# Matmuls without a result in TensorE's waits between stages, and one PSUM bank kept out of the ring

## The reference

```python
def first_block(x, mem, ...):
    h = x
    for l in range(2):
        proj = rms_norm(h, norm_mix_pre[l]) @ w_in[l]
        ...  # dilated window attention, short convolution, gated delta rule
        mix = jnp.concatenate([y_attn, y_conv, y_gdn], axis=-1) @ w_out[l]
        h = h + rms_norm(mix, norm_mix_post[l])
        hn = rms_norm(h, norm_xattn_pre[l])
        xa = memory_cross_attention(hn, rms_norm(mem, norm_mem[l]), w_xq[l], w_xkv[l], w_xo[l])
        h = h + rms_norm(xa, norm_xattn_post[l])
        hn = rms_norm(h, norm_ffn_pre[l])
        h = h + rms_norm(swiglu_ffn(hn, w_gate_up[l], w_down[l]), norm_ffn_post[l])
    return h

def second_block(x, c, ctx, ...):
    for i in range(2):
        h_lat = rms_norm_2(x_lat, norm_g[i]) * (1.0 + sc_l) + sh_l   # the same for ctx
        ...  # i = 0: two grouped attentions; i = 1: conformer convolution and neighbourhood attention
        x_lat = x_lat + g_l * y_lat
    return rms_norm_2(x_lat, final_g)
```

## Time and profile before

| | us |
|---|---|
| median of three runs | 2859.71 (2857.09 to 2866.64) |
| profiled execution | 2864.18 |
| its span, first to last instruction | 2862.4 |
| PE busy | 2629.6 (92%) |
| DVE busy | 1673.3 (58%) |
| ACT busy | 1134.4 (40%) |
| mean clock granted to PE, of full speed | 0.941 |

### The profile page before, as it was taken

The page is one execution under the profiler, slowest core; times in us unless marked ns, Lnnn a source line. Parts: engine busy times, 40 slices in busy tenths (PEclk is TensorE's granted clock), DMA queues, the critical chain, the costliest instruction groups (busy, mean ns, idle before and its releaser), DMA issues.

```text
span 2862.4 us, 34696 instructions
## 1 busy us (share of the span) xinstructions
PE 2629.6 (92%) x13264; PEld 2107.0 (74%) x13264; DVE 1673.3 (58%) x3236; ACT 1134.4 (40%) x2071; POOL 0.2 (0%) x4
## 2 busy tenths in 40 slices
PE   7998899989999799898899899997989997899888
PEld 5876888668888578687876688886866666787556
DVE  6655565455446875565643644576376674398653
ACT  4235443433322332454444332323346673322562
POOL 0000000000000000000000000000000000000000
PEclk9989999989999899899999899996999998799898
DMA  4310033113226423101321232452110001122311
GB/s 146 99 52 16 2 118 111 43 65 98 96 98 220 139 81 99 38 1 45 120 87 57 69 96 96 161 192 92 52 37 16 23 16 33 34 81 67 69 43 45
DMA packets 73364, 218.33 MB, mean 76 GB/s; under 512 B 21232, under 2 KB 21488, under 8 KB 72560
## 3 DMA queue, kind: packets, MB, share of 16 engines
q1 hardware_dynamic: 48384, 176.29, 19.0%
q10 hardware_dynamic: 24816, 39.82, 4.4%
HBM read 213.98 MB, written 2.10 MB: 75 GB/s over the span
## 4 chain that ended last, share of the span: by engine, by line
PE 75%; DVE 13%; ACT 6%; issue 5%; DMA 1%; ACTq 1%; DVEq 0%; SPq 0%
PE bank L574 19%; PE bank L575 18%; PE bank L576 18%; PE bank L765 4%; PE bank L729 3%; DVE mod_part L2396 3%; PE bank L739 3%; ACT w_hi L533 2%; PE bank L1588 2%; PE bank L1183 1%; DVE w_lo L540 1%; PE bank L1191 1%; DVE hT L700 1%; PE bank L1129 1%; DVE y_x L693 1%
## 5 line engine op out<-in xcount | busy, mean ns | idle before, releaser
L574 PE MATMUL bank<-a_hi,w_hi 128*128 128x512 f32 (+1 forms) x1552 | 623.9, 402 | 43.5 <-ACT a_hi L603 21.7
L575 PE MATMUL bank<-a_lo,w_hi 128*128 128x512 f32 (+1 forms) x1552 | 613.1, 395 | 0.0
L576 PE MATMUL bank<-a_hi,w_lo 128*128 128x512 f32 (+1 forms) x1552 | 612.5, 395 | 0.0
L540 DVE TENSOR_TENSOR w_lo<-w_raw,w_hi 128x1024 fp32r<-128x1024 f32 x334 | 407.7, 1224 | 305.6 <-ACT w_hi L533 304.5
L533 ACT ACTIVATE w_hi<-w_raw 128x1024 fp32r<-128x1024 f32 x334 | 352.4, 1060 | 579.3 <-PE bank L576 486.5
L574 PEld LDWEIGHTS bank<-a_hi,w_hi 128*128 128x128 f32 (+1 forms) x1552 | 295.0, 190 | 132.6 <-issue 47.8
L576 PEld LDWEIGHTS bank<-a_hi,w_lo 128*128 128x128 f32 (+1 forms) x1552 | 295.1, 190 | 65.1
L575 PEld LDWEIGHTS bank<-a_lo,w_hi 128*128 128x128 f32 (+1 forms) x1552 | 295.2, 190 | 63.5 <-issue 3.0
L574 PE MATMUL bank<-b_hi,w_hi 128*128 128x512 f32 (+1 forms) x800 | 299.9, 375 | 36.0 <-DVE b_lo L713 23.5
L575 PE MATMUL bank<-b_lo,w_hi 128*128 128x512 f32 (+1 forms) x800 | 289.3, 362 | 0.0
L576 PE MATMUL bank<-b_hi,w_lo 128*128 128x512 f32 (+1 forms) x800 | 287.3, 359 | 0.0
(11 more groups left out here) (364 smaller groups left out, 3770.2 us busy)
## 6 DMA issues: line engine op xcount, KB each, us to landing
w_raw<-w_tiles SPq DMA_DIRECT2D x334, 512.0 KB, 3.4
mod_raw<-mod_tiles ACTq DMA_DIRECT2D x48, 512.0 KB, 3.5
d_bias<-rpb_rows ACTq DMA_DIRECT2D x16, 224.0 KB, 4.7
hT<-xT ACTq DMA_DIRECT2D x4, 512.0 KB, 11.2
m_in<-memT ACTq DMA_DIRECT2D x2, 1024.0 KB, 4.7
mod_cond<-cond_rows ACTq DMA_DIRECT2D x2, 1024.0 KB, 5.3
out<-hT ACTq DMA_DIRECT2D x8, 256.0 KB, 2.2
cT<-ctxT ACTq DMA_DIRECT2D x1, 1024.0 KB, 6.7
```

Of the source, the lines that this page charges most:

```text
L540: dve.tensor_tensor(w_lo[:, t % SPLIT, :], w_raw[:, t % RAW, :], w_hi[:, t % SPLIT, :].bitcast(f32), ALU.subtract).then_inc(sem("w_split"), 1)
L574: pe.matmul(o, wh, hi[:, k, :n], start=k == 0, stop=False)
L575: pe.matmul(o, wh, lo[:, k, :n], start=False, stop=False)
L576: mm = pe.matmul(o, wl, hi[:, k, :n], start=False, stop=k == kc - 1)
```

## The change

A helper `warm_pe(pe, n, key)` is added: it claims a bank, issues n plain f32 matmuls of 128 x 512 from two constant tables into it, and frees the bank itself with the last one; nobody reads the bank. It is called from twelve lines of PE's stream, 76 matmuls in all: in each of the two layers of the first block 1 ahead of the sums of `x_post`, 1 ahead of its broadcast, 5 behind it; 3 ahead of the sums of `f_post`, 1 ahead of its broadcast, and behind it 5 in layer 0 and 3 in layer 1; in the second block 3 ahead of the even input products, 9 ahead of the even attention, 13 ahead of the even output products, 3, 8 and 10 at the same places of the odd layer. Apart from this the bank of `rstd_pe` of `mix_post` is now held from its claim until product 11 of the memory has been issued.

```diff
+        def warm_pe(pe, n, *key):
+            b = claim(pe, "warm", *key)
+            for _ in range(n):
+                mm = pe.matmul(b[:, :], ident, con[:, 0:512], start=True, stop=True)
+            mm.then_inc(*freed("warm", *key))
...
-        def rstd_pe(pe, key, n):
+        def rstd_pe(pe, key, n, hold=False):
             pe.wait_ge(*when("spread", *key))
-            b = claim(pe, "rstd", *key)
+            b = claim(pe, "rstd", *key, hold=hold)
...
         def second_pe(pe):
             mod_norm_pe(pe, 0)
+            warm_pe(pe, 3, "even_in")
             even_in_pe(pe)
+            warm_pe(pe, 9, "even_att")
             attention_pe(pe, ("even",), even_units(), e_s, pair_tiles(e_pt), even_values,
...
+            warm_pe(pe, 13, "even_out")
             even_out_pe(pe)
             mod_norm_pe(pe, 1)
+            warm_pe(pe, 3, "odd_in")
             odd_in_pe(pe)
             conformer_pe(pe)
             odd_turn_pe(pe)
+            warm_pe(pe, 8, "odd_att")
...
+            warm_pe(pe, 10, "odd_out")
...
                 if c == 2:
-                    rstd_pe(pe, ("mix_post", l), S)
+                    rstd_pe(pe, ("mix_post", l), S, hold=True)
+                if c == KC + 3:
+                    book.release("rstd", "mix_post", l)
...
+                warm_pe(pe, 1, "x_post", l)
                 ssq_pe(pe, ("x_post", l), S)
+                warm_pe(pe, 1, "x_rstd", l)
                 rstd_pe(pe, ("x_post", l), S)
+                warm_pe(pe, 5, "f", l)
                 ffn_pe(pe, l)
+                warm_pe(pe, 3, "f_post", l)
                 ssq_pe(pe, ("f_post", l), S)
+                warm_pe(pe, 1, "f_rstd", l)
                 rstd_pe(pe, ("f_post", l), S)
+                warm_pe(pe, 5 if l + 1 < DEPTH else 3, "mix", l + 1)
```

## The result

The changed kernel takes 2835.4 us in the median of four runs (2833.1 to 2837.8), against 2860.3 (2857.1 to 2866.6, four runs) before: ratio 0.991, 95% interval 0.989 to 0.993. The execution profiled took 2833.24, with a span of 2831.4 and a mean clock of 0.966 instead of 0.941; the stretches at 0.50 are 25 with 195 us in all, before 33 with 341. The forecast clock was 0.955.

A forecast was written before the change was run, and what follows sets the result against it. PE, 92% busy at mean clock 0.941, was taken to be bound by its waits and critical-path stretches at the lower clock. 2864.2 less 28.9 (16.5 + 3.7 + 3.2 + 1.2 + 1.3 + 3.0) less 3.5 gave 2831.8 us, range 2821 to 2848.

The forecast's parts named there:

- The bank: Memory products: holding the bank ends PE's wait before product 10; 8.2 us gained in layer 0, 8.3 in layer 1, together 16.5.
- The wait that I put at 0.65 us: Memory product 13: PE would wait 0.65 us for DVE's weight split, subtracted from the layer's gain.
- Rival B: Memory products: the bank wait becomes a wait for DVE's split at 3.5 us a product; 6 us less gain, 2838, chance 0.13.
- `x_post` and `f_post`: Three places, not layer 1's `f_post`: faster sums and broadcasts gain 4.6 us, discounted to 3.7; the following passes gain nothing.
- The border: `f_post` of layer 1 into block two: 1.2 us from sums, 0.7 from the load, 1.3 from even input products, 3.2 gained.
- Even output: Start of even output products: 13 fillers keep the clock up in a wait of 13.38 us; 1.3 us gained.
- Odd output: Start of odd output products: 10 fillers keep the clock up in a wait of 10.14 us; 3.0 us gained.
- Odd attention: Start of odd attention: 8 fillers hidden in the wait, PE then waits for DVE's bias work; gain nothing.
- Luck: Whole profiled execution: 4.5 us above the runs' median, 3.5 of it put down to badly landed clock falls and subtracted.
- my clock terms: Filler gains: norms 3.7 us, border 3.2, even attention 1.2, even output 1.3, odd output 3.0.
- Rival D: The 48 sums at the border stay at full clock to their end; 8 us more gain, 2824, chance 0.04.
- Rival E: Fillers run at 1.2 GHz, outlast their waits and hold up queued work; slower, 2880, chance 0.04.

## Why the prediction was right, and where it was not

**The bank: right in mechanism and size.** 8.00 and 7.90 us for 8.2 and 8.3, and the kernel with the bank alone shows the same without fillers. The wait that I put at 0.65 us is 0.41, at the product where I put it, and product 12 ahead of it takes 3.51 us from start to start instead of 2.88. Rival B's 3.5 us for each product are out: products 10 to 15 take 18.2 us, not 21. By medians this part is 14 (9 to 19) of the 22 to 25 us.

**`x_post` and `f_post`: right where PE is on the path.** Sums and broadcasts run fast, 0.95, 1.76 and 1.20 us gained, for 1.4, 1.9 and 1.3 before the discount, and the clock falls again in the gated passes. The five places together gain 4.85 and 3.25 us in the two profiles, but 2.1 also without fillers, since the passes ran faster in that one: the fillers' part is 1.2 to 2.8, not 3.7. That the fives cost nothing was right; that they gain nothing either is what the run without them adds.

**The border: 3.2 forecast, 1.3 in the first profile, 4.2 in the second.** "They will start fast and then fall" fails in the first: behind the three fillers PE waits 2.90 us for the context, the clock falls at 1941.8, and the sums start at 1942.4. The load of the context took 7.7 us from issue to landing instead of 6.7 and ate the 0.8 gained ahead of it. In the second the sums do start fast and then fall, and gain 2.3 us for my 1.2. Of five profiles with these three fillers and unchanged sums it is the only one; in the other four the clock falls between 0.6 us ahead of the first record and 0.5 behind it. So the mechanism was possible and its size luck. The 1.5 us of the even input products come with the bank alone too: in the profile of before a stretch at 0.50 (2007.9 to 2011.3) lay there, and I counted its end as gain of the fillers.

**Even output: 1.3 forecast, 0.4 measured, and 0.3 without fillers.** I took 1.3 of a 2.1 us loss, since the pause left over might let the clock fall. It did in both profiles: a fall 0.9 us behind the first pass costs as much as one ahead of it.

**Odd output: 2.83 for 3.0**, with 1.36 us of pause and no fall, and 2.84 in the second profile. With the bank alone the place is 1.6 us slower than in the changed kernel, with the short one-column fillers 2.9, so the clock's luck has a part in this size too.

**Odd attention: 0 forecast, 1.33 measured, and 1.58 and -0.32 in two kernels without these fillers.** The stretches at 0.50 lie differently there in each profile, so this place shows no gain of the fillers, as forecast, and could hide one of about 1 us.

**Luck: mis-sized.** Pooled over all rounds the kernel before has a median near 2858, so the profiled 2864.2 was 6 us unlucky, not 3.5. And my clock terms (12.4 us for all fillers) were read off this execution, so they counted part of that bad luck as gain: on top of the bank the fillers are worth 6 to 8 by the runs, 5 and 6 by the table (the two profiles of the changed kernel less that of the bank alone). This is the term of the sum that was wrong, by nearly a factor of two. The two errors are of opposite sign, 2.4 and, with the fillers put at 7, 5.4; with 0.6 from the bank they leave the 3.6. That the forecast came so near is in part luck.

**Rival D** (the sums stay fast) is out in the sharpest form: 30 us of one-column matmuls without a pause ran at 0.50 to their end, and with wide ones between them the same sums ran at 1.00. The rule of the Trainium skill that I weighed (TensorE: Matmul & The Clock Gate, section "HAM oscillation — how this bites in real kernels"), which names pauses as what makes the clock fall, doesn't cover these rows, in which PE had none. At the even output the fall does come with a pause (2.03 us, six profiles of seven). **Rival E** is out: the four large groups run at full clock, 11.43 us for the 13, and end ahead of their waits. Only the threes behind the slow broadcasts of the second block are late (3.6 and 4.0 us), and the first pass behind them starts no later for it.

## What to carry to other kernels

Read a stretch at the lower clock together with what sets the pace in it: 31 of the 76 matmuls, those just ahead of the sums and broadcasts of `x_post` and `f_post`, of the even attention and of the odd output, did all that could be measured, and where DVE feeds the passes the clock hardly matters. A buffer that a ring hands on while it is still read is worth a look first, since holding one bank took away a wait of 6 us twice, without any luck. And before a matmul without a result is added, see whether a needed one can be made wide: the sums with the ones as stationary operand gained 9 us in two norms and some 13 in three, all fillers 6 to 8.

## What the runs showed of the hardware

- A one-column f32 matmul takes two records of 0.12 us at full clock and two of 0.22 at 0.50, a 128 x 512 one 0.86 us in all: 512 columns for under four times the price of one.
- Keeping PE busy is not enough: 143 records of one column filled 30.2 of 30.2 us, at 0.50. With a wide matmul behind every eight (or, of 256 columns, every four) such records the clock was 1.00 for 23 us.
- The same kernel spreads over 17 us from run to run before (2851 to 2868, some 50 runs), over 7 after (2833 to 2840, nine runs). The two profiles of the changed kernel differ in where the clock falls; that this explains the spread before, of which there is one profile, is not shown.
- One load of 1024 KB, the context's, took 4.8 to 8.5 us from issue to landing in the fourteen profiles, 6.7 in the kernel before; why is open.
- DVE's reciprocal takes 3.35 us for 128 x 512 and 1.70 to 1.75 for 128 x 256, about four times a scale of that shape (0.75 and 0.48).
